# Placing every large stage tensor of a float32 two-block transformer kernel at the same start address modulo 512 bytes as its inputs and weight parts

## The reference, cut to what matters

```python
def first_block(x, ...):                 # layer 0 and layer 1
    h = x
    h = h + stick_breaking(rmsnorm(h) @ w_qkv) @ w_o
    h = h + swiglu(rmsnorm(h), w_gate, w_up, w_down)      # hidden width 2816
    kv = rmsnorm(h) @ w_kv                                # another gain than q's
    h = h + dilated_attention(rmsnorm(h) @ w_q, kv) @ w_o
    h = h + swiglu(...)
    return rmsnorm(h)

def second_block(x, ...):
    h = layer_norm(ALPHA * h + hgrn2_mixer(h))            # gated linear recurrence, 8 heads
    h = layer_norm(ALPHA * h + conv_ffn(h))               # hidden width 2816
    h = layer_norm(ALPHA * h + windowed_attention(h))
    return layer_norm(ALPHA * h + conv_ffn(h))
```

## Time and profile before

| | |
|---|---|
| median of 3 runs | 2487.62 us (2486.83 to 2491.34) |
| profiled execution, time | 2489.66 us |
| profiled execution, span from first to last instruction | 2487.8 us |
| PE busy | 2435.3 us (98%), 11652 matmuls |
| PEld busy | 1977.5 us (79%) |
| DVE busy | 1399.1 us (56%) |
| ACT busy | 908.1 us (37%) |
| POOL busy | 168.5 us (7%) |
| mean granted TensorE clock | 0.996 |
| HBM traffic | 88 GB/s over the span |

### The profile page before, as it was taken

The page is one execution under the profiler, slowest core; times in us unless marked ns, Lnnn a source line. Parts: engine busy times, 40 slices in busy tenths (PEclk is TensorE's granted clock), DMA queues, the critical chain, the costliest instruction groups (busy, mean ns, idle before and its releaser), DMA issues.

```text
span 2487.8 us, 31250 instructions
## 1 busy us (share of the span) xinstructions
PE 2435.3 (98%) x11652; PEld 1977.5 (79%) x11652; DVE 1399.1 (56%) x2268; ACT 908.1 (37%) x1295; POOL 168.5 (7%) x179
## 2 busy tenths in 40 slices
PE   8999999999999999999999999999999999999998
PEld 6777888888777788888788887788888877888886
DVE  5665655533766465542266765766642665766634
ACT  5443322222656332222332332533321564433312
POOL 0000000000000000000020000000030462000031
PEclk9999999999999999999999999999999999999999
DMA  4212323223112232322321112223223312333232
GB/s 146 66 62 82 96 93 100 85 93 101 60 60 77 76 103 93 99 78 93 106 81 67 51 67 93 85 93 97 88 86 108 128 52 82 97 95 99 80 114 85
DMA packets 60791, 218.94 MB, mean 88 GB/s; under 512 B 6773, under 2 KB 7061, under 8 KB 60576
## 3 DMA queue, kind: packets, MB, share of 16 engines
q1 hardware_dynamic: 58608, 208.74, 26.2%
q0 software_dynamic: 2064, 8.97, 1.1%
q10 hardware_dynamic: 32, 0.02, 0.0%
HBM read 215.59 MB, written 2.12 MB: 88 GB/s over the span
## 4 chain that ended last, share of the span: by engine, by line
PE 90%; DVE 5%; ACT 4%; issue 1%; DMA 0%; POOL 0%; DVEq 0%; SPq 0%; ACTq 0%
PE ps L254 27%; PE ps L256 27%; PE ps L255 27%; PE ps L1820 2%; PE ps L1000 2%; PE ps L1026 1%; PE ps L1012 1%; ACT window_p L1488 1%; DVE wl L248 1%; ACT wh L240 1%; PE ps L1844 0%; DVE window_p L1550 0%; PE ps L1034 0%; DVE stick_left L1199 0%; PE ps L1841 0%
## 5 line engine op out<-in xcount | busy, mean ns | idle before, releaser
L254 PE MATMUL ps<-xh,wh 128*128 128x512 f32 x2000 | 797.0, 399 | 16.9 <-DVE xl L460 7.6
L256 PE MATMUL ps<-xh,wl 128*128 128x512 f32 x2000 | 781.7, 391 | 0.0
L255 PE MATMUL ps<-xl,wh 128*128 128x512 f32 x2000 | 780.6, 390 | 0.0
L240 ACT ACTIVATE wh<-raw 128x1024 fp32r<-128x1024 f32 x332 | 349.3, 1057 | 495.7 <-PE ps L256 475.2
L248 DVE TENSOR_TENSOR wl<-raw,wh 128x1024 fp32r<-128x1024 f32 x332 | 409.6, 1236 | 195.7 <-ACT wh L240 195.2
L254 PEld LDWEIGHTS ps<-xh,wh 128*128 128x128 f32 x2000 | 377.1, 189 | 99.5 <-issue 14.0
L256 PEld LDWEIGHTS ps<-xh,wl 128*128 128x128 f32 x2000 | 376.6, 188 | 80.3
L255 PEld LDWEIGHTS ps<-xl,wh 128*128 128x128 f32 x2000 | 377.4, 189 | 76.3 <-issue 2.2
L254 PE MATMUL ps<-wh,up_ah 128*128 128x512 f32 x528 | 208.6, 395 | 1.0 <-DVE wl L404 1.0
L255 PE MATMUL ps<-wl,up_ah 128*128 128x512 f32 x528 | 208.3, 395 | 0.0
L256 PE MATMUL ps<-wh,up_al 128*128 128x512 f32 x528 | 208.3, 395 | 0.0
(11 more groups left out here) (269 smaller groups left out, 3051.1 us busy)
## 6 DMA issues: line engine op xcount, KB each, us to landing
raw<-weights SPq DMA_DIRECT2D x388, 512.0 KB, 3.6
cst<-rows_d POOLq DMA_DIRECT2D x9, 512.0 KB, 4.9
hT<-x_t SPq DMA_DIRECT2D x8, 256.0 KB, 6.1
hgrn_mask<-levels POOLq DMA_DIRECT2D x1, 2048.0 KB, 7.7
window_bias<-bias_rows POOLq DMA_DIRECT2D x1, 2048.0 KB, 9.4
out_t<-hT SPq DMA_DIRECT2D x8, 256.0 KB, 2.2
cst<-consts SPq DMA_DIRECT2D x1, 832.0 KB, 8.7
cvt<-conv SPq DMA_DIRECT2D x1, 176.0 KB, 8.6
```

Source lines behind the costliest of these rows:

```text
L240: act.activation(wh[slot][:, :], raw[slot][:, :], ACT.Copy).then_inc(hi_done, 1)
L254: pe.matmul(out, w_hi, m_hi, start=first, stop=False, **kw)
L255: pe.matmul(out, w_hi, m_lo, start=False, stop=False, **kw)
L256: return pe.matmul(out, w_lo, m_hi, start=False, stop=last, **kw)
```

## The change

It moves tensors in SBUF and does nothing else. Every engine has the same instructions in the same order, with the same semaphores; only addresses in them differ. Before, the resident tensors up to `wl` started at 128 modulo 512 bytes (`hT` starts at byte 16512 = 32 x 512 + 128, and the sizes from `hT` to `wl` are multiples of 512). `base` was the next multiple of 128, byte 118272 = 231 x 512 + 0. Now resident tensors whose sizes are multiples of 512 are allocated first, `base` gets the remainder of `hT`, and the `Arena` rounds up to a multiple of 512 from `base` ahead of each tensor of 512 bytes or more.

```diff
+LINE = 512
...
+        lead = (nc.sbuf_base + (-nc.sbuf_base) % 32) % LINE
         hT = sb("hT", [P, KT, S])
         xh = sb("xh", [P, KT, S], F32R)
         xl = sb("xl", [P, KT, S], F32R)
         raw = [sb(f"raw{k}", [P, SLAB]) for k in range(SLOTS)]
         wh = [sb(f"wh{k}", [P, SLAB], F32R) for k in range(SLOTS)]
         wl = [sb(f"wl{k}", [P, SLAB], F32R) for k in range(SLOTS)]
+        cst = sb("cst", [P, max(CONST_COLS, P + 2 * D)])
+        ones = sb("ones", [P, P])
+        rstd = sb("rstd", [P, S])
+        acc = sb("acc", [P, S])
+        cvt = sb("cvt", [P, 2, 2 * FT, 4])
         vec = sb("vec", [P, VEC_COLS])
-        cst = sb("cst", [P, max(CONST_COLS, P + 2 * D)])
-        cvt = sb("cvt", [P, 2, 2 * FT, 4])
-        ones = sb("ones", [P, P])
         small = sb("small", [P, 8])
         tiny = sb("tiny", [P, 16])
         grow, brow = cst[:, P:P + D], cst[:, P + D:P + 2 * D]
-        rstd = sb("rstd", [P, S])
-        acc = sb("acc", [P, S])
...
-        base = nc.sbuf_base + (-nc.sbuf_base) % 128
+        base = nc.sbuf_base + (lead - nc.sbuf_base) % LINE
...
         class Arena:
...
+                if n >= LINE:
+                    self.at += -self.at % LINE
```

## The result

The changed kernel takes 2474.02 us as the median of 6 runs (2471.24 to 2475.77), the kernel before 2488.68 us in the same comparison (6 runs, 2486.83 to 2491.34). The ratio is 0.9939, with a 95% interval of 0.9926 to 0.9952. So the three comparisons give 14.7 to 18.7 us.

The account below looks back on a forecast made before the run. PE, busy 98% of 2487.8 us, bounds the kernel. Faster stage products sum to 15.6 to 17.8 us, taken as 16.7, other parts as nothing: 2487.6 − 16.7 = 2470.9 us, chance 0.87; range 2466 to 2477 us.

Parts of the forecast that it names:

- the window output as a control: Window stage output: same code, roles and shapes as down2, but equal remainders; 227.3 ns a matmul against 232.4.
- no change: Whole kernel: the 5 ns belong to something other than the remainder, so time stays 2487.6 us; chance 0.06.
- down1 to down3: Products of form `Tok` in three down stages: 1584 matmuls faster by 5.6 ns each, saving 8.9 us.
- down0: Products of form `Out` in this stage: 528 matmuls faster by 6.6 ns each, saving 3.5 us.
- dilated output: Output products of the dilated attention stage: 192 matmuls faster by 6.6 ns each, saving 1.3 us.
- dilated keys and values: Products with `x2h` in the dilated stage: 384 matmuls faster by 5 ns each, saving 1.9 us.
- the rival at 7.8 us of gain: Down stages: PE waits for weights, losing 8.9 us of saving; 2479.8 us. Chance 0.03, or 0.05 with its other half.
- its other half: Float32r products: only one of the forms `Out` and `Tok` answers to the remainder, giving a similarly reduced gain; included in 0.05.
- the up to 2 us: Some 700 float32 transposes on PE: equal remainders may cost up to 3 ns each, 0 to 2 us; taken as 0.
- the rival that ended slower: Float32 transposes suffer from equal remainders, from 31 ns each over 5 us slower: 2493 us or more; chance 0.02.
- one stretch of 3.4 us: Whole kernel: a stretch of granted clock at 0.50 lasts 3.4 us and costs 1.7 us.
- ten new ones: Whole kernel: new low-clock stretches, 1.7 us each, said to be needed for a slower result; held no way there.

Follow-up runs that it names:

- the three comparisons: Changed kernel against the kernel before, 14.7 us less; the changed kernel again, 18.7 us less; changed kernel with `base` 256 bytes further, 18.1 us less.
- base_only: Kernel before with only `base` put at remainder 128 modulo 512, which moves window tensors from 128 to 256: 2473.07 us, ratio to before 0.9931.
- residents_only: Changed kernel's new order of resident tensors, stage tensors left at 0 as before: 2490.81 us against 2491.02 of before, ratio 1.0001.
- the second: Comparison in which the changed kernel ran again unedited: 2471.99 us against 2490.70 of before, ratio 0.9930.

## Why the prediction was right

**The cause.** "So the question is whether a matmul's pace depends on where its two operands lie": it does. The step that carried the prediction, the window output as a control with the same code and other addresses, was confirmed from the other side by `base_only`, which slowed exactly that stage. The rival "no change" is out. The Trainium skill, page "SBUF — State Buffer", section "Who interferes with whom", calls PE's two read ports independent. The traces of this case do not agree: at most distances between the starts of PE's two operands a matmul takes 5 to 8 ns more than at 0. Where in the chip the two reads meet was not tested.

**The sum.** By the rows: down1 to down3 1584 x 5.7 = 9.0 us (said 8.9), down0 528 x 6.6 = 3.5 (3.5), stick output 6.2 x 192 = 1.2 (1.1), dilated output 6.1 x 192 = 1.2 (1.3), hgrn output 4.8 x 192 = 0.9 (1.1), dilated keys and values 4.2 ns (from all starts) x 384 = 1.6 (1.9). That is 17.4 us by long runs. All intervals together give 17.1, and 16.7 without what the clock took from the dilated output before, against 16.7 forecast. That the two agree to a tenth is luck: the long runs gained their full price and the short groups less than said. The two smaller than said are those with short groups of matmuls between plain float32 matmuls.

**Does the saving reach the end?** Weights did not become the wait: the waits of PE for `wl` from L252 come to 3.1 us against 3.0, the one wait in down3 stayed (1.1 us against 1.0), and down2 has none. So the rival at 7.8 us of gain is out, and since both forms sped up, so is its other half. Transposes did not mind equal remainders; timeline of PE in the hgrn stage of the changed kernel, for the earlier trace rows:

```profile
1293.29 0.60 PE L1897 MATMUL ps<-cst,hgrn_vs 128*128 128x128 f32 x4
1297.85 1.05 PE L1822 MATMUL ps<-hgrn_Q,hgrn_KG 128*128 128x128 f32 x8
```

They take 0.60 us for four, as before, and from start to start the transposes of `hT` and of the probabilities take 109.1 or 109.2 ns in all twelve traces. So the up to 2 us that the prediction kept for them in its range did not come, and the rival that ended slower is out. `cst` at 128 instead of 160 is read by DVE in 689 ns (was 691), and `residents_only` found no gain in that half of the change.

**What the prediction left out** is how much the clock moves a single execution. It knew one stretch of 3.4 us at the price of 1.7 us and took the stretches as they were. In fact their number and length, and the rise of the clock at the start, differ between executions by 1 to 2 us each. (Its "ten new ones" would only cancel the saving; to end 5 us slower takes thirteen.) In the first comparison the three executions of the changed kernel with a mean granted clock of 0.996 took 2474.7 to 2475.8 us, the three with 0.997 took 2471.2 to 2473.4; in the second, one had 0.996 (2475.1) and four 0.997 (2471.0 to 2472.5). That goes with most of the 2.0 us between the two medians, 2474.0 and 2472.0; the median of before moved by 2.0 the other way. The forecast gain of 16.7 us lies between the two measured gains of 14.7 and 18.7.

**What was not foreseen** is the unit. The prediction spoke of equal remainders modulo 512, as the change does; the rows of before had only distances of 0 and 384, and could not tell 512 from 256.

## What to carry to other kernels

When two groups of the same matmul differ by a few nanoseconds in one profile, list the start addresses of both operands beside the groups: it was a stage that lay differently by accident (two tensors of 64 bytes ahead of the others) that pointed to the cause before any run. For float32r matmuls of 512 columns, the only kind that was slowed here, place what PE streams and what it loads so that their starts agree modulo 256 bytes. Here one number where an arena begins does it (`base_only`), and it is worth 0.6 to 0.7% of a kernel that PE bounds. Judge PE by the distance of starts over a long run, not by durations or busy share, which stood at 98% in both kernels; and sum the intervals of the affected matmuls before reading a gain of 0.7% off one span, which the clock moves by some microseconds.

## What the runs showed of the hardware that I had not expected

- The pace of back-to-back float32r matmuls of 512 columns depends on (moving start − stationary start) modulo 256 bytes: 226.7 ns at 0, 228.8 at 64, 232 to 234 at every other multiple of 32 tried.
- Matmuls of 256 columns did not pay at the one distance tried: 119.9 ns at distance 0 and 120.0 at 128.
- A stationary part at an unequal remainder slows two matmuls, the one during which it is loaded and the one that uses it (5.7 and 7.6 ns in down2); a moving one slows only its own (7.4 ns in down0).
- Even at distance 0 the first ten or so float32r matmuls after a plain float32 one start up to 236 ns apart before they settle at 226.7. The `xh` matmuls of hgrn and window, which run in short groups, have means of 230.2 and 228.1 ns in the changed kernel (waits left out), against 226.7 in up0 to up3. Why they need this long is open.
- Plain float32 transposes of 128 columns take 109 ns from start to start in all twelve traces, wherever their operands start.
